# DeltaNet recurrence in nine steps instead of eight, odd heads one chunk behind even heads, with all its products as 64x64 tiles of two heads

## What is computed

```python
def step(state, inp):
    q_i, k_i, u_i, w_i, a_i, g_i = inp
    v_new = u_i - w_i @ state
    o = (q_i * exp(g_i)) @ state + a_i @ v_new
    state = state * exp(g_last) + (k_i * exp(g_last - g_i)).T @ v_new
    return state, o
```

## Time and profile before

| what | value |
|---|---|
| time, median of 3 runs (range) | 1889.99 us (1889.91 to 1894.7) |
| profiled execution | 1890.07 us, span 1888.3 us |
| PE busy | 1858.6 us (98% of the span) |
| DVE, ACT, POOL busy | 898.5, 448.9, 1032.4 us |
| chain that ended last | PE 90%, DVE 7%, issue 1%, ACT 1% |
| lower and corner products with their k-steps | 21.65 us a layer |
| recurrence, to the first gate matmul | 44.98 us in layer 0, 44.97 in layer 1 |

### The profile page before, as it was taken

How to read it: one execution, slowest core, us unless ns; L and a number is a source line. 1 busy time by engine, 2 the same in 40 slices (tenths; PEclk the granted TensorE clock), 3 DMA queues, 4 the chain that set the end, 5 groups by cost and what they waited for, 6 DMA issues and landing times.

```text
span 1888.3 us, 26079 instructions
## 1 busy us (share of the span) xinstructions
PE 1858.6 (98%) x9980; PEld 1511.8 (80%) x9980; DVE 898.5 (48%) x1375; ACT 448.9 (24%) x788; POOL 1032.4 (55%) x580
## 2 busy tenths in 40 slices
PE   7999999999999999999999999999999999999998
PEld 6887788668888888888888778886788888888887
DVE  6687545664354323223266855466535542314141
ACT  6333213441113000000154233153501220000010
POOL 5543166326566666666654523662356666667662
PEclk9999999999999999999999999999999999999999
DMA  6222023113233323333342211330222323333322
GB/s 221 81 62 68 23 90 101 56 31 127 90 91 113 96 93 101 95 95 101 100 135 68 68 57 35 100 101 28 86 90 90 100 90 100 100 94 96 100 91 76
DMA packets 46759, 167.06 MB, mean 88 GB/s; under 512 B 5018, under 2 KB 8346, under 8 KB 46146
## 3 DMA queue, kind: packets, MB, share of 16 engines
q1 hardware_dynamic: 44066, 154.30, 26.3%
q10 hardware_dynamic: 2592, 11.29, 1.6%
HBM read 159.28 MB, written 6.29 MB: 88 GB/s over the span
## 4 chain that ended last, share of the span: by engine, by line
PE 90%; DVE 7%; issue 1%; ACT 1%; DMA 0%; POOL 0%; SPq 0%; ACTq 0%; DVEq 0%; POOLq 0%
PE ps L420 26%; PE ps L422 25%; PE ps L421 25%; PE ps L832 2%; PE ps L854 1%; DVE lanes L1582 1%; PE ps L842 1%; PE ps L638 1%; PE ps L645 1%; PE ps L669 1%; DVE ps L1598 1%; PE ps L494 1%; DVE outer L1595 1%; DVE acc L1371 1%; DVE negmax L1787 1%
## 5 line engine op out<-in xcount | busy, mean ns | idle before, releaser
L395 POOL TENSOR_SCALAR wHi<-wraw 128x1024 fp32r<-128x1024 f32 x288 | 308.2, 1070 | 803.8 <-PE ps L422 790.2
L397 POOL TENSOR_TENSOR wLo<-wraw,wHi 128x1024 fp32r<-128x1024 f32 x288 | 724.2, 2515 | 24.0
L420 PE MATMUL ps<-hHi,wHi 128*128 128x512 f32 x1376 | 554.1, 403 | 4.6 <-POOL wLo L397 2.6
L422 PE MATMUL ps<-hHi,wLo 128*128 128x512 f32 x1376 | 537.2, 390 | 0.0
L421 PE MATMUL ps<-hLo,wHi 128*128 128x512 f32 x1376 | 536.9, 390 | 0.0
L420 PEld LDWEIGHTS ps<-hHi,wHi 128*128 128x128 f32 x1376 | 259.1, 188 | 68.8 <-issue 11.4
L422 PEld LDWEIGHTS ps<-hHi,wLo 128*128 128x128 f32 x1376 | 258.7, 188 | 55.3
L421 PEld LDWEIGHTS ps<-hLo,wHi 128*128 128x128 f32 x1376 | 259.2, 188 | 49.5 <-issue 1.4
L420 PE MATMUL ps<-fHi,wHi 128*128 128x512 f32 x640 | 249.3, 389 | 0.0
L422 PE MATMUL ps<-fHi,wLo 128*128 128x512 f32 x640 | 249.0, 389 | 0.0
L421 PE MATMUL ps<-fLo,wHi 128*128 128x512 f32 x640 | 249.0, 389 | 0.0
(11 more groups left out here) (289 smaller groups left out, 2030.0 us busy)
## 6 DMA issues: line engine op xcount, KB each, us to landing
wraw<-stream SPq DMA_DIRECT2D x288, 512.0 KB, 3.5
out<-xT ACTq DMA_DIRECT2D x2, 2048.0 KB, 8.2
xT<-out ACTq DMA_DIRECT2D x2, 2048.0 KB, 9.0
xin<-x SPq DMA_DIRECT2D x4, 512.0 KB, 6.0
out<-ost ACTq DMA_DIRECT2D x1, 1024.0 KB, 4.2
out<-ost ACTq DMA_DIRECT2D x2, 512.0 KB, 3.8
prm<-params ACTq DMA_DIRECT2D x1, 647.0 KB, 4.0
prm<-params SPq DMA_DIRECT2D x1, 576.0 KB
```

Source lines behind the costliest of these rows:

```text
L395: nc.gpsimd.tensor_scalar(wHi[:, slot], wraw[:, raw], 1.0, 0.0, ALU.mult, ALU.add).then_inc(unit_high, 1)
L397: nc.gpsimd.tensor_tensor(wLo[:, slot], wraw[:, raw], wHi[:, slot].bitcast(F32), ALU.subtract).then_inc(unit_split, 1)
L420: mm(o, lh[lc], rh[rc], start=start, stop=False)
L422: return mm(o, ll[lc], rh[rc], start=False, stop=stop)
```

## The change

Step s of nine now works on chunk s of the even heads and chunk s - 1 of the odd heads (`chains`), so that the two heads of a pair are in opposite halves of the partitions in each product. All products of the recurrence become 64x64 tiles, even and odd head in turn: the two of a pair use different row halves and different column halves of the array, and write different partition halves of the same bank. k @ state goes to the left half of S(2) and the product with the inverse to its right half; q @ state comes behind k @ state in place of the k-step; the state is 64 wide (no zero blocks), and its update is one DVE operation; r and the output copy become two operations each. av tile 1 is spread over steps 0 to 6, av tile 2 is projected as a whole behind the recurrence, and `turn_delta_output(0)` stands in step 7. In the lower and corner products the two parities alternate product by product, in two groups of 32 products, with four k-steps behind each. `scale_z(2)` comes behind all four transposes. Two of three memsets go. The decay factors of odd heads are written one column further (two ACT operations in place of one). In `corner_products` the loops change as in `lower_products`; that part, the counts of the semaphores and, in `recur`, the removed lines are left out below; leading blanks are cut too.

```diff
+def chains(step):
+    return [(par, step - par) for par in range(2) if 0 <= step - par < CHUNKS]
...
         upper, lower = at(60, "upper", [P, TT * HEADS, 32]), at(64, "lower", [P, TT * HEADS, 32])
-        r, vnew = at(56, "r", [P, 512]), [at(58, "vnew0", [P, 512]), at(92, "vnew1", [P, 512])]
-        state, sdec = at(88, "state", [P, PAIRS, P]), at(90, "sdec", [P, PAIRS, P])
+        r, vnew = at(56, "r", [P, PAIRS, 64]), at(58, "vnew", [P, 2, PAIRS, 64])
+        state, sdec = at(88, "state", [P, PAIRS, 64]), at(90, "sdec", [P, PAIRS, 64])
...
-    for group in range(4):
-        hf, ch = divmod(group, 2)
+    for hf in range(2):
         for n in range(16):
             g = 16 * hf + n
             tt, h = divmod(g, HEADS)
-            last = mm(S(2 + group)[64 * ch + 32:64 * ch + 64, 32 * n:32 * n + 32],
-                      gated[64 * ch:64 * ch + 32, tt, 0, h, 32:64], upper[64 * ch:64 * ch + 32, g], start=True, stop=True)
-        last.then_inc(lower_done, 1)
-        project(("z", 3), range(2 * group, 2 * group + 2))
+            for ch in range(2):
+                last = mm(S(2 + 2 * hf + ch)[64 * ch + 32:64 * ch + 64, 32 * n:32 * n + 32],
+                          gated[64 * ch:64 * ch + 32, tt, 0, h, 32:64], upper[64 * ch:64 * ch + 32, g], start=True, stop=True)
+        last.then_inc(lower_done, 2)
...
+def recur(step):
+    both = chains(step)
+    hs = lambda m: np.s_[64 * (m % 2):64 * (m % 2) + 64]
+    cs = lambda par: np.s_[64 * par:64 * par + 64]
+    if step == 0:
+        pe.wait_ge(corner_placed, layer * per.corner_placed + 2)
     else:
...
+        pe.wait_ge(state_done, layer * per.state_done + step)
+        if step == 1:
             pe.wait_ge(corner_placed, layer * per.corner_placed + 4)
...
+        else:
+            pe.wait_ge(o_copied, layer * per.o_copied + step - 1)
         for j in range(PAIRS):
...
+            for par, m in both:
+                if m:
+                    last = mm(S(2)[hs(m), j * 64:j * 64 + 64], kqe[cs(par), j, m // 2, m % 2, 0], state[cs(par), j], start=True, stop=True)
         last.then_inc(ws_done, 1)
...
+        for j in range(PAIRS):
+            for par, m in both:
+                if m:
+                    mm(S(step % 2)[hs(m), j * 64:j * 64 + 64], kqe[cs(par), j, m // 2, m % 2, 1], state[cs(par), j],
+                       start=j == 0, stop=False, skip_group_check=True)
+        pe.wait_ge(r_ready, layer * per.r_ready + step)
+    for j in range(PAIRS):
+        for par, m in both:
+            h = 2 * j + par
+            last = mm(S(2)[hs(m), 256 + j * 64:256 + j * 64 + 64], gated[hs(m), m // 2, 0, h],
+                      r[hs(m), j] if m else rhsv[hs(m), 0, h * 64:h * 64 + 64], start=True, stop=True)
     last.then_inc(tr_done, 1)
...
+    if step:
+        chunk_output(step - 1)
     else:
...
+        project(("av", 1), range(0, 1))
+    pe.wait_ge(vnew_done, layer * per.vnew_done + step + 1)
+    if step == CHUNKS:
+        chunk_output(step)
     else:
...
         for j in range(PAIRS):
...
+            for par, m in both:
+                if m < CHUNKS - 1:
+                    h = 2 * j + par
+                    last = mm(S(3)[cs(par), j * 64:j * 64 + 64], kend[hs(m), m // 2, h * 64:h * 64 + 64], vnew[hs(m), step % 2, j],
+                              start=True, stop=True)
+        last.then_inc(supd_done, 1)
+        if step < CHUNKS - 1:
+            project(("av", 1), range(step + 1, step + 2))
+        else:
+            turn_delta_output(0)
+def chunk_output(step):
+    for j in range(PAIRS):
+        for par, m in chains(step):
+            hs = np.s_[64 * (m % 2):64 * (m % 2) + 64]
+            last = mm(S(step % 2)[hs, j * 64:j * 64 + 64], gated[hs, m // 2, 1, 2 * j + par], vnew[hs, step % 2, j],
+                      start=m == 0 and j == 0, stop=j == PAIRS - 1, skip_group_check=True)
     last.then_inc(o_done, 1)
...
 corner_products()
-for m in range(CHUNKS):
-    recur(m)
-    if m == 6:
-        turn_delta_output(0)
+for step in range(CHUNKS + 1):
+    recur(step)
 turn_delta_output(1)
+project(("av", 2))
...
-def copy_output(m):
-    tt, ch = divmod(m, 2)
-    act.wait_ge(o_done, layer * per.o_done + m + 1)
-    nc.scalar.copy(o_tm[64 * ch:64 * ch + 64, tt], S(m % 2)[64:128]).then_inc(o_copied, 1)
-    if ch:
-        square_o(tt)
-for m in range(CHUNKS):
-    tt, ch = divmod(m, 2)
-    hs = np.s_[64 * ch:64 * ch + 64]
-    act.wait_ge(tr_done, layer * per.tr_done + m + 1)
-    nc.scalar.copy(vnew[ch][hs], S(2)[hs]).then_inc(vnew_done, 1)
-    if m in (4, 6):
-        root_o(tt - 2)
-    if m:
-        copy_output(m - 1)
+def copy_output(step):
+    act.wait_ge(o_done, layer * per.o_done + step + 1)
+    for par, m in chains(step):
+        rows = np.s_[64 * (m % 2):64 * (m % 2) + 64]
+        ins = nc.scalar.copy(o_tm[rows, m // 2].rearrange("p (j q v) -> p j q v", j=PAIRS, q=2)[:, :, par],
+                             S(step % 2)[rows, 0:256].rearrange("p (j v) -> p j v", j=PAIRS))
+    ins.then_inc(o_copied, 1)
+    if step and step % 2 == 0:
+        square_o(step // 2 - 1)
+for step in range(CHUNKS + 1):
+    rows = np.s_[0:64] if step == 0 else np.s_[64:128] if step == CHUNKS else np.s_[0:128]
+    act.wait_ge(tr_done, layer * per.tr_done + step + 1)
+    nc.scalar.copy(vnew[rows, step % 2].rearrange("p j v -> p (j v)"), S(2)[rows, 256:512]).then_inc(vnew_done, 1)
+    if step in (5, 7):
+        root_o((step - 5) // 2)
+    if step:
+        copy_output(step - 1)
 root_o(2)
-copy_output(CHUNKS - 1)
+copy_output(CHUNKS)
 root_o(3)
...
     ins = nc.vector.transpose(heads_of(g, 0).rearrange("p t h s -> p s t h"), xt[rows].transpose([0, 2, 1]))
     if g % 2 == 0:
         ins.then_inc(inv_placed, 1)
-    if g == 3:
-        scale_z(2)
+scale_z(2)
 scale_z(3)
-nc.vector.memset(vnew[0][64:128], 0.0)
-nc.vector.memset(vnew[1][0:64], 0.0)
-nc.vector.memset(state[:], 0.0).then_inc(state_zero, 1)
+nc.vector.memset(state[64:128], 0.0).then_inc(state_zero, 1)
 take(avT[:, 0], ("av", 0))
 def sum_o(tt):
     dve.wait_ge(osq_ready, layer * per.osq_ready + tt + 1)
 dve.wait_ge(z_ready, layer * per.z_ready + 4)
 dve.wait_ge(state_zero, layer * per.state_zero + 1)
-for m in range(CHUNKS):
-    tt, ch = divmod(m, 2)
-    hs = np.s_[64 * ch:64 * ch + 64]
-    if m:
-        dve.wait_ge(ws_done, layer * per.ws_done + m)
-        tt_(r[hs], rhsv[hs, tt], S(m % 2)[0:64], ALU.subtract).then_inc(r_ready, 1)
-    if 0 < m < CHUNKS - 1:
-        dve.wait_ge(state_done, layer * per.state_done + m)
-        tt_(sdec[:], state[:], eglb[:, :, m:m + 1].broadcast_to([P, PAIRS, P]), ALU.mult).then_inc(sdec_done, 1)
-    if m == 4:
-        take(avT[:, 1], ("av", 1))
-    if m in (3, 5, 7):
-        sum_o(tt - 1)
-    if m in (5, 7):
-        scale_o(tt - 2)
-    if m == 7:
+by_pair = lambda t: t.rearrange("p (j v) -> p j v", j=PAIRS)
+for step in range(CHUNKS + 1):
+    if step:
+        dve.wait_ge(ws_done, layer * per.ws_done + step)
+        for par, m in chains(step):
+            if m:
+                hs = np.s_[64 * (m % 2):64 * (m % 2) + 64]
+                ins = tt_(r[hs], rhsv[hs, m // 2].rearrange("p (j q v) -> p j q v", j=PAIRS, q=2)[:, :, par],
+                          by_pair(S(2)[hs, 0:256]), ALU.subtract)
+        ins.then_inc(r_ready, 1)
+    if 0 < step < CHUNKS:
+        dve.wait_ge(state_done, layer * per.state_done + step)
+        tt_(sdec[:], state[:], eglb[:, :, step:step + 1].broadcast_to([P, PAIRS, 64]), ALU.mult).then_inc(sdec_done, 1)
+    if step in (4, 6, 8):
+        sum_o((step - 4) // 2)
+    if step in (6, 8):
+        scale_o((step - 6) // 2)
+    if step == CHUNKS:
         gate_o(0)
-    if m < CHUNKS - 1:
-        if m:
-            dve.wait_ge(sdec_done, layer * per.sdec_done + m)
-        for part in range(2):
-            pairs, upd = np.s_[2 * part:2 * part + 2], S(3 + 2 * part).rearrange("p (j n) -> p j n", j=PAIRS)
-            dve.wait_ge(supd_done, layer * per.supd_done + 2 * m + part + 1)
-            for block in (np.s_[0:64, pairs, 0:64], np.s_[64:128, pairs, 64:128]):
-                if m:
-                    ins = tt_(state[block], sdec[block], upd[block], ALU.add)
-                else:
-                    ins = nc.vector.tensor_copy(state[block], upd[block])
-        ins.then_inc(state_done, 1)
+    else:
+        dve.wait_ge(supd_done, layer * per.supd_done + step + 1)
+        if step:
+            rows = np.s_[64:128] if step == CHUNKS - 1 else np.s_[0:128]
+            dve.wait_ge(sdec_done, layer * per.sdec_done + step)
+            tt_(state[rows], sdec[rows], by_pair(S(3)[rows, 0:256]), ALU.add).then_inc(state_done, 1)
+        else:
+            nc.vector.tensor_copy(state[0:64], by_pair(S(3)[0:64, 0:256])).then_inc(state_done, 1)
+take(avT[:, 1], ("av", 1))
 scale_o(2)
-take(avT[:, 2], ("av", 2))
 gate_o(1)
 sum_o(3)
+take(avT[:, 2], ("av", 2))
 gate_o(2)
 scale_o(3)
 gate_o(3)
```

(23 more changed lines are left out.)

30 lines of the change are left out of this document (6 added, 24 removed).

## The result

| | before | after |
|---|---|---|
| time, median of 6 runs each (range) | 1892.22 us (1889.91 to 1894.77) | 1901.47 us (1898.24 to 1907.73) |
| profiled execution, span | 1890.07 us, 1888.3 us | 1901.43 us, 1899.6 us |
| clock over the span | 0.999 | 0.996 |

The ratio is 1.0058, interval 1.0045 to 1.0072: slower by 0.6%, where 0.6% faster was forecast. 1901.47 us lies 23.3 us over the forecast and 12.5 over the end of its range. The runs of the kernel before stand in two groups, near 1890.0 and 1894.6 us, so that its median here lies between them; against the lower group, from which the forecast was worked out, the kernel after is 11.5 us slower.

The account below looks back on a forecast made before the run. PE was taken to bound the kernel, with 90% of the chain. Recurrence -2.39 and lower and corner products -3.53 make -5.92 us a layer, -11.8 for two, from 1890.07 to 1878.2 us; range 1874 to 1889.

Parts of the forecast that it names:

- At no cost: Edits outside the two changed stretches were taken as free; the eglb exponent would cost some 0.3 us if uncovered.
- shared-bank rival: Recurrence: two tiles writing one bank run in sequence; 1897.6 us, or 1902.2 with 32x32 tiles in sequence too; chance 0.15.
- Start distance across tiles: Lower and corner products: full overlap, 1.12 us to the k-step; by the 25 ns floor, 2.4 us more in all, 1880.6.
- Links: Recurrence, one full step: products to r 1.60 us, inverse products to v_new 1.20, update to next state products 1.49.
- longer links: Rival, recurrence: DVE operation 0.68 us and v_new copy 0.58 whatever the columns; 1887.5 us; chance 0.07.
- half overlap: Rival, recurrence: paired tiles start together but run slower than one alone; 1888 us at half the loss; chance 0.07.
- One step 4.29: Recurrence: a full step takes 4.29 us, against 5.82 before.
- The root, +0.97: Recurrence: ACT's table load and root in step 5 delay output copies that step 6 awaits, adding 0.97 us.
- Step 7, 4.39: Recurrence: step 7 takes 4.39 us, as sdec ends 0.41 behind POOL's split, instead of 3.98 without it.
- Recurrence 42.59: The nine steps and av tile 2 sum to 42.59 us a layer, against 44.98: -2.39.
- Lower and corner products 18.12: Groups of 4.11 us (before 5.42) plus 1.7 of PE idle for ACT's copies; -3.53 a layer.
- The clock: Rival, recurrence: PE idling drops it to 1.2 GHz, some 20 us a layer; chance 0.03.

Follow-up runs that it names:

- a_order: `a_aligned` with `scale_z(2)` moved back to its earlier place among the transposes; 1874.92 us, ratio 0.9927 against the kernel before.
- a_aligned: Kernel after with 32 bytes less ahead of the `at` tiles, so that they begin where they did before; 1883.42 us, ratio 0.9964 against the kernel before.
- r_only: Kernel after with old lower and corner products, old `scale_z(2)` place and old address, leaving the new recurrence alone; 1888.68 us, ratio 0.9990 against the kernel before.
- a_fill: `a_order` with av tile 2 spread over the steps, a k-step in PE's gap before `r`; 1874.6 us, ratio 0.9914 against the kernel before.
- a_best: `a_fill` with ACT's table for the root loaded ahead of the recurrence; 1871.61 us, ratio 0.9905 against the kernel before.
- g_only: Kernel before with only the new lower and corner products, `scale_z(2)` and addresses as before; 1882.33 us, ratio 0.9953.
- b_shift32: Kernel before with its `at` tiles 32 bytes further on, nothing else changed; 1908.93 us, ratio 1.0097.

## Why the prediction was wrong

**The step that failed is "At no cost", the eglb exponent.** It was costed as "one small ACT operation more", and its only other cost given as 0.3 if uncovered. The operation was free: `a_order`, which has it too, begins its first lower products at 167.65, against 167.70 before. The column that it writes into was not: it made a tile 16 bytes wider, the rounding made that 32, and 2496 matmuls of unchanged work ran 6 ns longer. The sum had a term for each edited instruction and none for the bytes that an edited declaration moves. None of the four rivals held it either; the 1897.6 and 1902.2 of the shared-bank rival are near the measured time by chance.

Point by point:

- *Tiles in one bank, on different partitions, overlap*: right. Pairs start 0.00 to 0.01 us apart. The shared-bank rival, and the Trainium skill's rule under which it stood ("TensorEngine Tiling (Array Packing)", Restrictions and Gotchas), don't hold for two row tiles that write different partitions of a bank.
- *Start distance across tiles*: 64 instructions of 32x32 span 1.20 us in the corner group, where one quadrant's 32 took 1.19. The floor of some 25 ns under any start-to-start distance ("TensorE: Matmul & The Clock Gate", Part 1, the Trainium skill) would ask 63 x 25 ns = 1.6 us, an estimate; the trace disagrees.
- *Links*: `r` takes 0.85 for its two operations (0.84 forecast), the copy of v_new 0.37 (0.44). The three parts of a step, forecast 1.60 + 1.20 + 1.49, took 1.64 + 1.15 + 1.50, so that small errors cancel in it. The rivals of longer links and of half overlap fall.
- *One step 4.29*: measured 4.29 to 4.31. Step 0: 3.00 against 2.98; step 1: 3.85 against 3.87.
- *The root, +0.97*: state products of step 5 at 206.11 and of step 6 at 211.24, 5.13, so +0.84.
- *Step 7, 4.39*: 4.68, from 215.52 to 220.20. `sdec`, 2.59 us, ended 0.28 behind POOL rather than 0.41, but later in the step: POOL began 1.42 us after the state products instead of 1.14.
- *Recurrence 42.59*: 42.73 in after, 42.71 in `a_aligned`, `r_only` and `a_order`. *Lower and corner products 18.12*: 18.26, with 1.88 of idle for the 1.7 forecast. Terms too small by 0.14 each, 0.6 us over both layers.
- *The clock*: the rival was given 0.03 and a price of some 20 us a layer. It came in the kernel after, but as single falls and not for the whole recurrence: 2.9 and 1.6 us. Its chance was too low and its price too high by the same mistake, of taking it for all or nothing.

The account of the 23.3 us between forecast and result, from the profiled execution: 17.2 in the two untouched stretches, by the address; 4.5 for the clock; 0.6 for the terms; and 0.9 outside the windows above, 0.4 ahead of the first lower product and 0.5 behind the last projection (9.20 us to the end against 8.72), which no run settles.

## The clock, as far as the rows go

The kernel after in layer 1, PE alone, as the clock falls and comes back among the corner products:

```profile
1114.82 0.64 PE L623 MATMUL ps<-gated,lower 32*32 32x32 f32 x29
1115.39 0.51 PE L425 MATMUL ps<-hHi,wHi 128*128 128x512 f32 x1
1115.72 0.60 PE L426 MATMUL ps<-hLo,wHi 128*128 128x512 f32 x1
1116.12 0.63 PE L427 MATMUL ps<-hHi,wLo 128*128 128x512 f32 x1
...
1119.11 0.42 PE L425 MATMUL ps<-hHi,wHi 128*128 128x512 f32 x1
```

The starts are 0.40 to 0.43 apart in between (0.23 at full clock): the lower of the two levels, 1.2 GHz, for 3.4 us. In layer 0 it lasted 6.8 us at a granted clock of 0.50:

```profile
221.40:228.20 6.80, 6.80 (x44) 6.00 (x45) 5.01 (x9) 2.60 (x7) 0.00 (x0) 0.50 0.16 63
```

The same kind of stretch stands at 221.8 in `a_aligned`, at 1105.8 there and at 1152.6 in `r_only`: at the end of a recurrence whose steps leave PE idle for 4.4 of 42.7 us, or 1.4 us behind the end of the wait of 1.9 for ACT. In the profiled executions of the kernel before, of the new lower and corner products alone, and of `a_order`, `a_fill` and `a_best`, no such stretch lies in or near the changed parts. `a_order` has the same idle time in its recurrence as `r_only` and kept the clock in its profiled execution, so the idle time alone doesn't decide it. Whether filling the gaps kept the clock up in `a_best` isn't settled by one profile each: one of its five runs lies 4.3 us above the median at a granted clock of 0.997, as one of the five of `a_order` lies 6.2 above.

Such stretches aren't the change's alone. The profiled executions have one early on too, at a granted clock of 0.50: 3.4 us of it from about 16 us on in the kernels before and after, and 6.8 us in `g_only`, where the lower products begin 1.5 us later than before. In `a_fill` and `b_shift32` 6.8 us of it come from 48.5 and 52.1 us on instead, and these two executions are the slowest of their kernels, 3.4 and 6.0 us above the medians; `a_fill` begins its first lower products 4.7 us later than `a_order`. So part of the spread between runs of one kernel arises ahead of anything that was changed, and a difference of some 5 us between two single executions by itself says nothing of the change.

## What to carry to other kernels

A diff moves data as well as work: before costing its operations, add up what each changed declaration does to the addresses of the tiles behind it, and after the run look at the mean time of instructions that nobody touched. As far as the seven starts run here go, streamed operands of the large matmuls should start at a multiple of 256 bytes in the partition, held there by a pad, so that a small tile can grow without moving them. Where PE bounds the kernel, an operation's place in DVE's order can cost nearly what a rewrite saves (`scale_z(2)` here, 1.9 us a layer, against 2.3 for the whole new recurrence).

## What the runs showed of the hardware that was not expected

- A matmul of 128x512 (fp32r operands) takes 389 ns with its streamed operand at a multiple of 256 bytes and 393 to 399 at 32, 96 or 128 bytes past one, for the same program. Over 2496 of them that is 15 us of 1890 at 32 bytes, where moving the tiles costs 17 to 19 in all.
- Two 64x64 tiles in different row and column halves run fully side by side into one bank, each on its own half of the partitions: 16 instructions span 0.68 us where one quadrant takes 1.14.
- A DVE operation with both inputs in SBUF that starts behind a POOL split ends shortly after it in the three cases seen, and takes several times its own time: 0.28 us after at 128x256 (2.59, against 0.43 alone), 0.54 and 0.55 at 128x512 (2.22 and 2.26, against 0.69). The Trainium skill, "SBUF — State Buffer", section "SBUF: two separate sides", has it as an exclusive lock on ports that the two engines share, for which the later one blocks; the trace agrees, 217.03 + 2.59 = 219.62 against POOL's end at 219.34, though the 0.28 between them is less than the operation's own 0.43.
